# First layer type without stage ends, with work moved between VectorE, ScalarE and TensorE's queue

## What is computed

```python
q_a = apply_axial_rope(rms_norm(q_a...), row_cs, col_cs)
o_att = block_attention(q_a, k_a, v_a)
o_hg = hgrn2_bidirectional(q_h, i_h, f_fw, f_bw, g_h, ...)
o_cv = conformer_conv(a_c, g_c, conv_w[l], ...)
x = x + jnp.concatenate([o_att, o_hg, o_cv], axis=-1) @ w_out[l]
```

## Time and profile before

| | us |
|---|---|
| median of 3 runs | 3802.38 |
| lowest and highest | 3798.88, 3803.84 |
| the profiled execution | 3799.13 |
| its span | 3797.8 |
| TensorE busy | 3651.8 (96%) |
| VectorE busy | 2161.4 (57%) |
| ScalarE busy | 1305.7 (34%) |
| GpSimd busy | 1197.6 (32%) |
| mean granted clock, share of full | 0.978 |

### The profile page before, as it was taken

One profiled execution on the slowest core, in us unless ns is written; L12 is line 12 of the kernel. 1 busy time (PEld: TensorE's weight loads), 2 busy tenths in 40 slices (PEclk: granted clock), 3 DMA queues, 4 the chain that ended last, 5 costly groups with the idle time before them and its releaser, 6 DMA issues.

```text
span 3797.8 us, 44671 instructions
## 1 busy us (share of the span) xinstructions
PE 3651.8 (96%) x17862; PEld 2808.5 (74%) x17862; DVE 2161.4 (57%) x3054; ACT 1305.7 (34%) x2217; POOL 1197.6 (32%) x486
## 2 busy tenths in 40 slices
PE   8889999998999999999999999999999999999998
PEld 6646888865588888676777678887767777778887
DVE  7787565688754474633374485545553255365445
ACT  6344121443522131544423532123354433342212
POOL 0002444200144443132333244444213232334443
PEclk9889999997999999999999999999999999999999
DMA  4101333320033333121222123334112222223332
GB/s 135 43 12 50 98 96 95 93 68 12 23 95 99 95 119 107 39 68 56 78 62 78 51 90 99 95 98 148 51 40 78 57 78 61 67 73 95 99 95 83
DMA packets 81373, 292.38 MB, mean 77 GB/s; under 512 B 9712, under 2 KB 11152, under 8 KB 80656
## 3 DMA queue, kind: packets, MB, share of 16 engines
q1 hardware_dynamic: 78384, 278.49, 24.0%
q10 hardware_dynamic: 2784, 11.03, 0.9%
HBM read 285.30 MB, written 2.10 MB: 76 GB/s over the span
## 4 chain that ended last, share of the span: by engine, by line
PE 85%; DVE 11%; issue 2%; ACT 2%; DMA 0%; SPq 0%; DVEq 0%; ACTq 0%
PE acc L334 23%; PE acc L336 22%; PE acc L335 22%; PE banks L929 2%; PE banks L648 2%; PE banks L604 2%; DVE conv_c L1307 2%; PE banks L631 2%; PE banks L940 1%; DVE stat L728 1%; PE banks L1555 1%; DVE probs L739 1%; DVE QK L857 1%; DVE w_lo L247 1%; DVE pair L406 1%
## 5 line engine op out<-in xcount | busy, mean ns | idle before, releaser
L278 POOL TENSOR_TENSOR w_lo<-w_raw,w_hi 128x1024 fp32r<-128x1024 f32 x482 | 1197.4, 2485 | 2570.1 <-ACT w_hi L231 2570.1
L231 ACT ACTIVATE w_hi<-w_raw 128x1024 fp32r<-128x1024 f32 x518 | 548.9, 1060 | 1725.5 <-PE acc L336 1641.6
L334 PE MATMUL acc<-hH,w_hi 128*128 128x512 f32 x1776 | 730.9, 412 | 13.2 <-DVE sig L1940 6.6
L336 PE MATMUL acc<-hL,w_hi 128*128 128x512 f32 x1776 | 699.4, 394 | 0.0
L335 PE MATMUL acc<-hH,w_lo 128*128 128x512 f32 x1776 | 698.8, 393 | 0.0
L334 PEld LDWEIGHTS acc<-hH,w_hi 128*128 128x128 f32 x1776 | 337.9, 190 | 99.7 <-issue 25.3
L334 PE MATMUL acc<-H,w_hi 128*128 128x512 f32 x1024 | 400.4, 391 | 3.8 <-DVE L L398 3.8
L369 DVE TENSOR_TENSOR xT<-acc,xT 128x512 f32<-128x512 f32 x160 | 110.7, 692 | 514.1 <-PE acc L336 495.6
L334 PE MATMUL acc<-midH,w_hi 128*128 128x512 f32 x1024 | 400.3, 391 | 0.3
L335 PE MATMUL acc<-midH,w_lo 128*128 128x512 f32 x1024 | 398.5, 389 | 0.0
L336 PE MATMUL acc<-midL,w_hi 128*128 128x512 f32 x1024 | 398.5, 389 | 0.0
(11 more groups left out here) (325 smaller groups left out, 4710.7 us busy)
## 6 DMA issues: line engine op xcount, KB each, us to landing
w_raw<-in_stream SPq DMA_DIRECT2D x518, 512.0 KB, 3.6
cw<-in_cmpw ACTq DMA_DIRECT2D x2, 2048.0 KB, 7.4
mixed<-in_cmpw ACTq DMA_DIRECT2D x2, 2048.0 KB, 12.7
x_tok<-in_x SPq DMA_DIRECT2D x2, 1024.0 KB, 7.4
out<-f_tok SPq DMA_DIRECT2D x8, 256.0 KB, 2.1
stack<-Z ACTq DMA_DIRECT2D x8, 128.0 KB, 2.3
stack<-Z ACTq DMA_DIRECT2D x8, 127.8 KB, 2.4
masks_f<-in_masks SPq DMA_DIRECT2D x1, 960.0 KB, 12.0
```

Source lines behind the costliest of these rows:

```text
L231: act.activation(w_hi[:, u % WB, 0:w], w_raw[:, u % 2, 0:w], ACT.Copy).then_inc(hi_split, 1)
L278: pool.tensor_tensor(w_lo[:, u % WB, 0:w], w_raw[:, u % 2, 0:w], w_hi[:, u % WB, 0:w], ALU.subtract)\
L334: pe.matmul(acc[n % 2][:, :], wh, H[:, k, :], start=(k == 0), stop=False)
L336: last = pe.matmul(acc[n % 2][:, :], wh, Lo[:, k, :], start=False, stop=(k == nk - 1))
```

## The change

No engine drains or waits for a whole stage in the first type. The transposes of the recurrence's values go to step 2 of run 0, those of the attention's values to step 1 of run 1. The far values (block pairs off the diagonal) are multiplied at step 17 of run 0 and step 13 of run 1, and only the diagonal pairs stand behind the last step. The recurrence's head norm is spread over step 9 and 11 of run 1 and slots 0 to 4 of the attention. The gaps of levels 256 and 128 are no longer made by VectorE: ScalarE subtracts the reference as the bias of its exponential, one instruction for each block, from a small row of negated references (`refs`). This holds for both layer types. In the first type, the probabilities of the pair's second head are scaled by ScalarE (`act_scale`). An output is taken a slot later (both types). The conv's taps are shared out by a list. Seven of the output's k steps (21 matmuls) go into slots 16 and 17, ahead of the last values.

The diff, cut to its core and with eight columns of indentation taken off:

```diff
...
+CONV_LATE = [2, 2, 1, 3, 1, 4, 4, 4, 4, 4, 3]
...
-def out_pe(layer, early, late, ready):
-    out_tiles = Group(layer, "out")
-    for ks in (early, late):
+def out_pe(layer, early, late, ready, out_tiles=None):
+    begun = out_tiles is not None
+    out_tiles = out_tiles or Group(layer, "out")
+    for ks in (late,) if begun else (early, late):
...
-def finish(eng, name):
-    done = {id(pe): pe_finished, id(act): act_finished, id(dve): dve_finished}[id(eng)]
-    eng.drain().then_inc(up(done), 1)
-def after(eng, stages, name, *who):
-    for done in who:
-        eng.wait_ge(done, since(done) + stages.index(name) + 1)
...
-            if side and slot < self.n:
+            if side:
...
-            pe.wait_ge(self.p_normed, since(self.p_normed) + 2 * s + a + 1)
+            if self.p_scaled is None:
+                pe.wait_ge(self.p_normed, since(self.p_normed) + 2 * s + a + 1)
+            elif a == 0:
+                pe.wait_ge(self.p_normed, since(self.p_normed) + 2 * s + 2)
+            else:
+                pe.wait_ge(self.p_scaled, since(self.p_scaled) + s + 1)
...
+            if self.p_scaled is not None and 1 <= slot <= self.n:
+                self.act_scale(slot - 1)
...
+    def act_scale(self, s):
+        m, pr = self.span(s)[2], self.P[:, s % 3, 1, 0:self.span(s)[2]]
+        act.wait_ge(self.p_normed, since(self.p_normed) + 2 * s + 1)
+        act.activation(pr, pr, ACT.Copy, scale=self.stat[:, s % 3, 2, 1:2]).then_inc(up(self.p_scaled), 1)
...
-            p = self.values_due(slot)
+            p = self.values_due(slot - 1)
...
+        if self.p_scaled is not None:
+            dve.reciprocal(rs, self.stat[:, s % 3, 1, :]).then_inc(up(self.p_normed), 1)
+            dve.wait_ge(self.p_normed, since(self.p_normed) + 2 * s + 1)
+            pr = self.P[:, s % 3, 0, 0:m]
+            dve.tensor_scalar(pr, pr, rs[:, 0:1], None, ALU.mult).then_inc(up(self.p_normed), 1)
+            return
...
+FIRST_TURN_BANKS = (4, 5, 5)
...
+        return self.steps[s][1] >= P
...
+        dve.tensor_scalar(self.refs[:, run, 0:self.dirs, 0:NT - 1], self.BB[run][:, :, P:T:P], -1.0, None, ALU.mult)\
+            .then_inc(up(refs_ready), 1)
         for s in range(self.n + 2):
-            if s < self.n and self.steps[s][1]:
+            if s < self.n and 0 < self.steps[s][1] < P:
                 d, h = self.steps[s]
...
+            d, h = self.steps[s]
+            if self.far(s):
+                act.wait_ge(refs_ready, since(refs_ready) + run + 1)
+                if s >= 2:
+                    act.wait_ge(terms_ready, since(terms_ready) + self.n * run + s - 1)
+            else:
+                act.wait_ge(gap_ready, since(gap_ready) + self.gaps(run, s) + 1)
             for which in range(2):
-                G = self.half(self.gap[:, s % 2, :], h, which)
-                last = act.activation(G, G, ACT.Exp, scale=1.0 if which else -1.0)
+                if self.far(s):
+                    for at in range(0, T, 2 * h):
+                        ref = (self.refs[:, run, d, (at + h) // P - 1:(at + h) // P] if which else
+                               self.BB[run][:, d, at + h:at + h + 1])
+                        c = at + which * h
+                        last = act.activation(self.gap[:, s % 2, c:c + h],
+                                              self.BB[run][:, d, 1 - d + c:1 - d + c + h], ACT.Exp,
+                                              scale=1.0 if which else -1.0, bias=ref)
+                else:
+                    G = self.half(self.gap[:, s % 2, :], h, which)
+                    last = act.activation(G, G, ACT.Exp, scale=1.0 if which else -1.0)
             last.then_inc(up(decay_ready), 1)
             if other and s >= 1:
...
+        steps = self.n if closes else 1 + max(s for s in range(self.n) if self.steps[s][1] >= P)
+        pe.wait_ge(level_kept, since(level_kept) + self.n * run + steps)
...
+        if not closes:
+            pairs = [(jt, it) for jt, it in pairs if jt != it]
+        elif not opens:
+            pairs = [(jt, it) for jt, it in pairs if jt == it]
         for j, (jt, it) in enumerate(pairs):
             for a, v, bank, rows in heads:
                 last = pe.matmul(bank[rows, it * P:(it + 1) * P], v(jt), self.block(a, jt, it),
-                                 start=(j == 0), stop=True, skip_group_check=True)
+                                 start=(opens and j == 0), stop=True, skip_group_check=True)
...
-            for n in (first_in.first + 10, first_in.first + 11):
-                pe.wait_ge(acc_free[n % 2], n // 2 + 1)
-            turn_pe([Z[:, 10, :], Z[:, 11, :]], 0)
-            pe.wait_ge(v_ready, since(v_ready) + 2)
...
+            def heads_of(r):
+                return [(a, lambda jt, a=a: v_tok[1 + r][:, jt, HD * a:HD * a + HD], B[4 + r],
+                         slice(HD * a, HD * a + HD)) for a in range(2)]
             def rope_pe(s):
+                if s == 17:
+                    pe.wait_ge(z_rstd, since(z_rstd) + 5)
+                    rec.pe_values(0, heads_of(0), closes=False)
+                if s == 2:
+                    for n in (first_in.first + 10, first_in.first + 11):
+                        pe.wait_ge(acc_free[n % 2], n // 2 + 1)
+                    turn_pe([Z[:, 10, :], Z[:, 11, :]], 0, FIRST_TURN_BANKS)
                 for t in range(5):
...
+                        if t == 0:
+                            pe.wait_ge(v_ready, since(v_ready) + 1)
...
+                        else:
+                            pe.wait_ge(v_ready, since(v_ready) + 2)
...
+            def second_run(s):
+                if s == 1:
+                    n = late_in.first + 5
+                    pe.wait_ge(acc_free[n % 2], n // 2 + 1)
+                    pe.wait_ge(z_done, since(z_done) + 5)
+                    turn_pe([Z[:, 5, :]], 2, FIRST_TURN_BANKS)
+                if s == 13:
+                    pe.wait_ge(v_ready, since(v_ready) + 3)
+                    rec.pe_values(1, heads_of(1), closes=False)
+                if s == 9:
                     pe.wait_ge(o_squared, since(o_squared) + 1)
                     pe.matmul(B[4][:, :], pair_ones, terms[:, 0, :], start=True, stop=True).then_inc(up(o_summed), 1)
-                    pe.wait_ge(z_done, since(z_done) + 5)
...
-            pe.wait_ge(o_squared, since(o_squared) + 2)
-            pe.matmul(B[5][:, :], pair_ones, terms[:, 1, :], start=True, stop=True).then_inc(up(o_summed), 1)
-            finish(pe, "hgrn")
-            after(pe, stages, "hgrn", act_finished, dve_finished)
-            turn_pe([Z[:, 5, :]], 2)
-            pe.wait_ge(v_ready, since(v_ready) + 3)
+            for r in range(2):
+                rec.pe(r, Z[:, 8 + r, :], both_keys[:, r, :], late_in, second_run if r else rope_pe)
+                rec.pe_values(r, heads_of(r), opens=False).then_inc(up(o_ready), 1)
...
+            def out_ready(k):
...
             def conv_pe(slot):
+                if slot == att.n:
+                    pe.wait_ge(conv_mean, since(conv_mean) + 2)
+                    pe.wait_ge(conv_rstd, since(conv_rstd) + 1)
+                    out_tiles.some(0, [4, 5, 0, 1], out_ready, True, False)
+                if slot == att.n + 1:
+                    out_tiles.some(0, [2], out_ready, False, False)
+                    out_tiles.some(1, [4, 5], out_ready, True, False)
+                if slot == 1:
+                    pe.wait_ge(o_squared, since(o_squared) + 2)
+                    pe.matmul(B[5][:, :], pair_ones, terms[:, 1, :], start=True, stop=True).then_inc(up(o_summed), 1)
+                    pe.wait_ge(o_rstd, since(o_rstd) + 1)
+                if slot == 4:
+                    pe.wait_ge(o_rstd, since(o_rstd) + 2)
...
-            finish(pe, "att")
-            pe.wait_ge(conv_mean, since(conv_mean) + 2)
-            pe.wait_ge(conv_rstd, since(conv_rstd) + 1)
...
-            out_pe(layer, [4, 5, 0, 1, 2], [3, 6, 7], out_ready)
+            out_tiles.some(1, [0, 1, 2], out_ready, False, False)
+            out_pe(layer, None, [3, 6, 7], out_ready, out_tiles)
...
-            turn_act([v_tok[1], v_tok[2]], 0)
...
+                if s == 3:
+                    turn_act([v_tok[1], v_tok[2]], 0, FIRST_TURN_BANKS)
...
+                if s == 2:
+                    turn_act([v_tok[0]], 2, FIRST_TURN_BANKS)
...
+                if s == 11:
+                    act.wait_ge(z_normed, since(z_normed) + 5)
+                    rstd_of_heads(0, tmp[:, :])
...
+            def rstd_of_heads(r, rs):
+                act.wait_ge(o_summed, since(o_summed) + r + 1)
+                link(act, act.activation(rs, B[4 + r][:, :], ACT.Ln, bias=EPS, scale=1.0 / HD))
+                act.activation(rs, rs, ACT.Exp, scale=-0.5).then_inc(up(o_rstd), 1)
...
+                n = FIRST_TILE[layer, "late_in"] + 6 + r
+                act.wait_ge(acc_free[n % 2], n // 2 + 1)
...
+            def conv_act(slot):
+                if slot == 0:
```

(28 more changed lines are left out.)

63 lines of the change are left out of this document (26 added, 37 removed).

## The result

The changed kernel takes 3826.2 us (median, 3820.67 to 3828.23) against 3801.0 us of the kernel before on the same chip: a ratio of 1.0063, 95% interval 1.0051 to 1.0074. It is slower by 25 us, where 38.5 us less were forecast, and the time lies outside the range given.

What follows compares the result with a forecast made beforehand. Taking TensorE, VectorE or chained small steps as bounds by stretch, with VectorE setting early attention, it summed gains of 17.5, 19.0 and twice 1.0 us over the layers to 38.5: 3764 us, range 3752 to 3782.

Steps and rivals of the forecast that it cites:

- beginning of run 0: First recurrence run's start: TensorE idles some 7.6 us, then pays a slow clock; loss 2.3 us in layer 0, 0.8 in layer 1.
- end of run 0: First recurrence run's end: far values fill TensorE's time between scores 16 and 17; gain 4.0 us a layer (1.7 to 5.5).
- run 1: Second recurrence run: inserted far values, transposes and sum over squares are partly absorbed by waits; loss 1.5 us (0 to 3.9).
- last level to last value: Second run's end: only 16 value records remain behind the last level, at 2.4 GHz; gain 5.0 us (2.5 to 5.4).
- stage end, to the first maximum: Between recurrence and attention: drains and waits go, first scores run at 2.4 GHz; gain 9.8 us (8.7 to 10.5).
- slots 0 to 10: Attention's first slots: VectorE sets the pace, saved scalings nearly offset added head work; loss 0.6 us (gain 0.5, loss 1.5).
- tail: Attention slots 11 to 18: TensorE and ScalarE set the pace, scaling delays ScalarE's copies; loss 0.4 us (gain 0.5, loss 1.5).
- output: Output products behind attention: 21 of 48 are done already, uncovering VectorE's conv split; gain 3.5 us (2.5 to 4.0).
- No row of POOL's or SP's queue changes its order: Layers 2 and 3: those queues keep their order, weight stream released up to 20 us sooner; 1.0 us gain each layer.
- Rival C: Slower: attention runs at 1.2 GHz, 1.9 us lost a slot, 61 us in 32 slots, so 3825 us; chance 0.04.
- One output taken a slot later, 1.3: Attention's first slots: taking one output a slot later removes 1.3 us from VectorE's time there.
- the outputs taken a slot later unblock VectorE: Layers 2 and 3: later outputs unblock VectorE, which had slack; with shorter gaps 1.0 us gain each (0 to 2).

Runs made afterwards that it cites:

- a_pad256: Changed kernel with the new tile refs at 256 bytes of a partition instead of 128, so later tiles keep their old distance from a multiple of 256; 3789.0 us.
- a_take_old: Changed kernel with refs at 256 bytes, each output taken by VectorE in the slot where its values are due, as before, in all four layers; 3778.2 us.
- a_gap_dve: Changed kernel with refs at 256 bytes, the eight far gaps of a layer back on VectorE; 3789.9 us.
- a_heads_first: Changed kernel with refs at 256 bytes, head-norm work back ahead of attention without drains or mutual engine waits, taps spread evenly; 3791.4 us.
- a_lead12: Changed kernel with refs at 256 bytes, value transposes back before run 0's first level, twelve parts of products ahead of it instead of three; 3766.4 us.

## Why the prediction was wrong

The terms of layer 0, by the trace of the changed kernel:

| term | forecast | measured | from |
|---|---|---|---|
| beginning of run 0 | -2.3 | -3.4 | third scores at 109.44, 106.06 before |
| end of run 0 | +4.0 | +3.4 | run 1 begins at 182.78, 182.76 before |
| run 1 | -1.5 | -1.6 | scores 17 at 220.71; 219.07 |
| last level to last value | +5.0 | +2.5 | 7.1 us; 9.56 |
| stage end, to the first maximum | +9.8 | +8.8 | 2.1 us; 10.9 |
| slots 0 to 10 | -0.6 | -5.3 | 53.8 us; 48.5 |
| tail | -0.4 | -0.6 | 31.1 us; 30.5 |
| output | +3.5 | +3.4 | 8.0 us; 11.4 |
| sum | +17.5 | +7.2 | |

Over the whole kernel, with the tiles back at their old place (the profiled executions of a_pad256 and of the kernel before, from one layer's first product on H to the next layer's): layer 0 gained 4.5 us where 17.5 were forecast, layer 1 gained 7.1 for 19.0, layer 2 lost 0.9 and layer 3 lost 2.7, where a gain of 1.0 each was forecast.

**What turned the sign** is in none of the terms. "No row of POOL's or SP's queue changes its order" and "TensorE is full there" were true of layers 2 and 3, and it was taken from them that untouched code keeps its time. This is the first step that failed. The prediction put untouched code at nothing, and it cost 40 us: a new tile moved the operands of 6912 matmuls. With the tiles at their old distance from a multiple of 256 bytes, the same change is 0.3% faster than the kernel before instead of 0.6% slower. Rival C forecast 3825 us and came within 2 us of the measured time by luck: it named another mechanism. Attention did run at 0.67 in its first slots, but a_pad256 has a like clock there and is faster than the kernel before. The reason the prediction gave against C was wrong too, "what brought it down is the 4.26 us wait that goes": without that wait the clock is 0.50 from 221.0 to 229.9. The Trainium skill (TensorE: Matmul & The Clock Gate, section HAM oscillation) says that broken-up work meets the half rate again and again; this trace agrees (0.67, then 0.86, where it had been 0.70, then 0.95), but of the time only the value slots' part can hang on it here.

**The step that failed among the terms** is "Attention slots 0 to 10. VectorE sets them" (loss 0.6, measured 5.3). VectorE's work was counted nearly rightly: from the first maximum to that of slot 11 it is busy for 48.4 us, 46.8 before. What was wrong is the waits: 1.7 us before, of which the prediction took 0.8 off, and 5.3 in the changed kernel. The sum takes every slot as bound by the same engine. In the value slots (6 and 10) TensorE's values stand ahead of the next scores; those slots took 6.5 and 5.5 us before and 6.7 and 6.2 after (from one reciprocal of VectorE to the next), though VectorE's load in them had fallen. Most of what was taken from there was worth nothing, and the output put into slot 7 cost 1.3 us (5.8 for 4.4; in slot 11, where VectorE waits too, it cost nothing). "One output taken a slot later, 1.3" was booked as a gain; it was the worst edit of the change, 11 us over four layers (a_take_old). In layers 2 and 3 the prediction had it as "the outputs taken a slot later unblock VectorE"; there it cost 7.5 of the 13 us by which the profiled executions differ. The far gaps, which shared the 1.0 us a layer with it, gave nothing (a_gap_dve).

**Stage end.** The price was right (8.8 of 9.8), and yet a_heads_first shows that most of it had no value: what hid behind TensorE's waits was VectorE's own 7.1 us, which the slots then had to carry. The prediction named this work and put it on the bill. What it lacked was the slots' shape.

**Last level to last value** was computed at 2.4 GHz; the clock was 0.50 (its own lower bound was 2.5, and that came). **Beginning of run 0** had the right mechanism and sign; the slow start lasted from 98.73 to some 105 us, longer than the "3 to 4 us" in the sum. What it missed is that 7.97 us without work are a place to fill: a_lead12 shows 23 us there, more than all that the change brought.
